# Roots of the key head norms, spread over the partitions by DMAs through a DRAM scratch in place of 16 selector products

## The reference, cut to what matters

```
def macaron_half(x, g, w_in, w_out):
    a, b = jnp.split(rms_norm(x, g) @ w_in, 2, axis=-1)
    return x + 0.5 * ((jax.nn.silu(a) * b) @ w_out)

def memory_kv(mem, g_mem, w_mkv, g_km):
    km, vm = jnp.split(rms_norm(mem, g_mem) @ w_mkv, 2, axis=-1)
    km = rms_norm(km.reshape(B, M, H_MEM, HEAD_DIM), g_km)
...
    k = rms_norm(k.reshape(B, S, H_A, 2, HEAD_DIM), p['g_k'])      # layer 0 keys, 12 heads of 64
...
    kb = rms_norm(kb.reshape(B, S, H_B, HEAD_DIM), g_kb)           # shared keys of layer 1, 12 heads of 64
```

## Time and profile before

| what | value |
|---|---|
| median of 3 runs | 1270.58 us (1270.34 to 1271.26) |
| span of the profiled execution, first to last instruction | 1269.0 us |
| PE busy | 1259.1 us, 99% |
| DVE busy | 753.9 us, 59% |
| ACT busy | 561.3 us, 44% |
| POOL busy | 187.3 us, 15% |
| DMA, mean rate over the span | 148 GB/s |

### The profile page before, as it was taken

How to read it: one execution, slowest core, us unless ns; L and a number is a source line. 1 busy time by engine, 2 the same in 40 slices (tenths; PEclk the granted TensorE clock), 3 DMA queues, 4 the chain that set the end, 5 groups by cost and what they waited for, 6 DMA issues and landing times.

```text
span 1269.0 us, 22398 instructions
## 1 busy us (share of the span) xinstructions
PE 1259.1 (99%) x8772; PEld 1241.4 (98%) x8772; DVE 753.9 (59%) x1135; ACT 561.3 (44%) x829; POOL 187.3 (15%) x206
## 2 busy tenths in 40 slices
PE   9999999999999999999999999999999999999999
PEld 8999999999998999999999999999997899999999
DVE  7766575555677656564555775554456765656433
ACT  6543453344276543433353443333355754343322
POOL 0120021146143000000122000001134420000000
PEclk9999999999999999999999999999999999999999
DMA  8364445643204443454443534354440134443343
GB/s 307 135 180 137 166 145 169 212 173 133 100 35 147 148 166 132 165 171 142 146 170 119 198 133 158 140 166 161 157 167 34 68 133 166 136 162 138 131 141 128
DMA packets 38829, 187.64 MB, mean 148 GB/s; under 512 B 4432, under 2 KB 13008, under 8 KB 23664
## 3 DMA queue, kind: packets, MB, share of 16 engines
q1 hardware_dynamic: 37296, 183.43, 41.7%
q0 software_dynamic: 1184, 3.13, 1.2%
q10 hardware_dynamic: 288, 0.24, 0.1%
HBM read 179.89 MB, written 6.90 MB: 147 GB/s over the span
## 4 chain that ended last, share of the span: by engine, by line
PE 97%; ACT 1%; DVE 1%; DMA 0%; issue 0%; SPq 0%; DVEq 0%; ACTq 0%
PE bank L504 30%; PE bank L506 30%; PE bank L505 30%; PE bank L918 1%; PE bank L780 1%; PE bank L741 1%; PE bank L783 1%; PE bank L750 1%; DMA raw<-in_w_ffn_in 0%; PE outs L530 0%; ACT ew L1321 0%; PE outs L532 0%; PE bank L552 0%; PE outs L817 0%; PE bank L545 0%
## 5 line engine op out<-in xcount | busy, mean ns | idle before, releaser
L504 PE MATMUL bank<-xhi,whi 128*128 128x320 f32 (+1 forms) x1760 | 545.8, 310 | 1.2 <-DVE wlo L1949 1.2
L506 PE MATMUL bank<-xhi,wlo 128*128 128x320 f32 (+1 forms) x1760 | 543.0, 309 | 0.0
L505 PE MATMUL bank<-xlo,whi 128*128 128x320 f32 (+1 forms) x1760 | 543.0, 309 | 0.0
L1562 DVE TENSOR_TENSOR wlo<-raw,whi 128x2048 fp32r<-128x2048 f32 (+1 forms) x176 | 361.5, 2054 | 235.7 <-ACT whi L1155 235.6
L1155 ACT ACTIVATE whi<-raw 128x2048 fp32r<-128x2048 f32 (+1 forms) x177 | 304.4, 1720 | 330.7 <-PE bank L506 325.0
L504 PEld LDWEIGHTS bank<-xhi,whi 128*128 128x128 f32 x1760 | 330.6, 188 | 3.7 <-issue 1.8
L505 PEld LDWEIGHTS bank<-xlo,whi 128*128 128x128 f32 x1760 | 330.7, 188 | 0.5
L506 PEld LDWEIGHTS bank<-xhi,wlo 128*128 128x128 f32 x1760 | 330.6, 188 | 0.0
L504 PE MATMUL bank<-hhi,whi 128*128 128x320 f32 x704 | 217.8, 309 | 0.0
L506 PE MATMUL bank<-hhi,wlo 128*128 128x320 f32 x704 | 217.5, 309 | 0.0
L505 PE MATMUL bank<-hlo,whi 128*128 128x320 f32 x704 | 217.5, 309 | 0.0
(11 more groups left out here) (236 smaller groups left out, 1051.7 us busy)
## 6 DMA issues: line engine op xcount, KB each, us to landing
raw<-in_w_ffn_in SPq DMA_DIRECT2D x85, 1024.0 KB, 4.8
raw<-in_w_ffn_out SPq DMA_DIRECT2D x64, 704.0 KB, 4.1
raw<-in_w_in_a SPq DMA_DIRECT2D x10, 1024.0 KB, 4.7
raw<-in_w_out SPq DMA_DIRECT2D x8, 1024.0 KB, 4.8
raw<-in_w_kv SPq DMA_DIRECT2D x6, 1024.0 KB, 4.7
raw<-in_w_mkv SPq DMA_DIRECT2D x4, 1024.0 KB, 4.8
raw<-in_w_in_b SPq DMA_DIRECT2D x4, 1024.0 KB, 4.8
raw<-in_w_ffn_in SPq DMA_DIRECT2D x6, 256.0 KB, 6.5
```

The lines of the kernel that those rows point to most:

```text
L504: mm(acc, wh, mhi(ks[q]), start=start and q == 0, stop=False)
L505: mm(acc, wh, mlo(ks[q]), start=False, stop=False)
L506: last = mm(acc, wl, mhi(ks[q]), start=False, stop=stop and q == nk - 1)
L1562: tt(wlo[slot][:, 0:size], raw[slot][:, 0:size], f32(whi[slot][:, 0:size]), ALU.subtract).then_inc(lo_ready[slot], 1)
```

## The change

The roots of the four sets of keys (`ROWS`: mkv0, mkv1, pa_k, kv) no longer pass through `rs` and PE. DVE writes them in full to `rt0`. ACT then issues one DMA that stores them in a DRAM scratch (`rows_to_memory`) and, after that has landed, two DMAs that read each row back onto 64 partitions (`rows_from_memory`). `head_scale` multiplies with that SBUF tile. `early_rows` lies in the buffer of `pt`, `late_rows` in the region of `qz`. A new semaphore `k_scaled` counts scaled key tiles. The stores of the memory keys and values wait for it and move in SP's order, and the scaling of the memory keys moves from d = 1 and 3 to d = 3 and 7 of `out0`.

```diff
+ROWS = {"mkv0": (0, 2, N_MEM), "mkv1": (1, 2, N_MEM), "pa_k": (2, 6, R), "kv": (3, 6, R)}
+SCALED = {"mkv0": 0, "mkv1": 2, "pa_k": 4, "kv": 10}
...
 (SP)
-            load_stage("out0", 0, 4)
-            for layer in range(2):
+            load_stage("out0", 0, 5)
+            def store_memory(layer):
                 st = f"mkv{layer}"
-                sp.wait_ge(aux_free, AUX0[st] + 4)
+                sp.wait_ge(k_scaled, SCALED[st] + 2)
+                sp.wait_ge(aux_free, AUX0[st] + 2)
                 store(a["o_mkT"][layer].rearrange("(k p) r -> p k r", p=P), kmT[:, layer])
                 store(a["o_mv"][layer].rearrange("(k p) r -> p k r", p=P), vm[:, layer])
-                if layer == 0:
-                    load_stage("out0", 4, 6)
+            store_memory(0)
+            load_stage("out0", 5, 6)
             sp.dma_start(ckT[:], a["cakT"]...)
             sp.dma_start(cv[:], a["cav"])...
             load_stage("out0", 6, 7)
...
             load_stage("out0", 7)
-            load_stage("pa")
+            load_stage("pa", 0, 1)
+            store_memory(1)
+            load_stage("pa", 1)
...
-            sp.wait_ge(aux_free, AUX0["dec"])
+            sp.wait_ge(k_scaled, SCALED["kv"] + 6)
             store(a["o_bkT"].rearrange("(k p) r -> p k r", p=P), kbT[:])
 (PE)
-                else:
-                    head_broadcast(st, AUX0[st] + 2, N_MEM)
...
-                if 11 <= j < 14:
-                    head_broadcast("pa_k", AUX0["pa_k"] + 2 * j - 22, R, [2 * j - 22, 2 * j - 21])
...
-                if i == 2 and j < 3:
-                    head_broadcast("kv", f + 7 + 2 * j, R, [2 * j, 2 * j + 1])
 (ACT)
+            def rows_to_memory(hn):
+                n, tiles, w = ROWS[hn]
+                act.wait_ge(hr_ready, HNORM[hn][0] + 1)
+                act.dma_start(rows_out[n, 0:2 * tiles, 0:w], rt0[0:2 * tiles, 0:w]).then_inc(d_rows_out, 16)
+
+            def rows_from_memory(hn):
+                n, tiles, w = ROWS[hn]
+                act.wait_ge(d_rows_out, 16 * (n + 1))
+                for e in range(2):
+                    src = bass.AP(rows_out.tensor, (12 * n + e) * R, [[0, HD], [2 * R, tiles], [1, w]])
+                    dst = rows_of(hn)[HD * e:HD * e + HD, :]
+                    act.dma_start(dst.rearrange("p (t r) -> p t r", t=tiles), src).then_inc(d_rows, 16)
...
+                       after=lambda j: rows_to_memory("mkv0") if j == 3 else None)
+            def memory_rows(d):
+                if d == 1:
+                    rows_from_memory("mkv0")
+                    head_root("mkv1", N_MEM)
+                if d == 3:
+                    rows_to_memory("mkv1")
+                if d == 5:
+                    rows_from_memory("mkv1")
...
+            def key_rows(hn):
+                def after(j):
+                    if j == 9:
+                        rows_to_memory(hn)
+                    if j == 10:
+                        rows_from_memory(hn)
+                return after
 (DVE)
                 val = tmp[0]
+                if hn in ROWS:
+                    stt(out=val[0:64, 0:w], in0=v, scalar=-3.0, in1=half, ...).then_inc(hr_ready, 1)
+                    return
...
+            def head_scale(hn, dst, g, tiles):
+                dve.wait_ge(d_rows, 32 * (ROWS[hn][0] + 1))
+                for j in tiles:
+                    stt(out=dst(j), in0=dst(j), scalar=g(j), in1=row_tile(hn, j), ...).then_inc(k_scaled, 1)
...
             def left_mkv(d):
+                if d in (3, 7):
+                    layer = d // 4
+                    head_scale(f"mkv{layer}", lambda j: kmT[:, layer, j, :], ..., range(2))
...
-                if 11 <= j < 14:
-                    head_scale("pa_k", ..., [2 * j - 22, 2 * j - 21])
+                if 13 <= j < 16:
+                    head_scale("pa_k", ..., [2 * j - 26, 2 * j - 25])
```

More of the change, by code:

```diff
@@ L82 @@
 AUX0 = {"mkv0": 0}
-AUX0["mkv1"] = AUX0["mkv0"] + 2 + 2
-AUX0["pa_k"] = AUX0["mkv1"] + 2 + 2
-AUX0["pa_q"] = AUX0["pa_k"] + 6
+AUX0["mkv1"] = AUX0["mkv0"] + 2
+AUX0["pa_q"] = AUX0["mkv1"] + 2
 AUX0["pa_v"] = AUX0["pa_q"] + 4
@@ L89 @@
 AUX0["kv"] = AUX0["pa_m"] + 2
-AUX0["dec"] = AUX0["kv"] + 1 + 6 + 1 + 6
+AUX0["dec"] = AUX0["kv"] + 1 + 6 + 1
+ROWS = {"mkv0": (0, 2, N_MEM), "mkv1": (1, 2, N_MEM), "pa_k": (2, 6, R), "kv": (3, 6, R)}
+SCALED = {"mkv0": 0, "mkv1": 2, "pa_k": 4, "kv": 10}
 AUX0["pb_m"] = AUX0["dec"] + 2
@@ L196, in encoder_kernel @@
         with ExitStack() as region:
+            sb("lower", [P, 8 * R], F32, region)
+            late_rows = sb("late_rows", [P, 6 * R], F32, region)
+        with ExitStack() as region:
             sb("under", [P, 4 * 640], F32, region)
@@ L215, in encoder_kernel @@
         idd = sb("idd", [P, HD])
+        early_rows = pt[:].rearrange("p a b -> p (a b)")
         hsq = sb("hsq", [P, R])
@@ L262, in encoder_kernel @@
         zT = qk[0:H_B, 13, :]
+        rows_out = nc.dram_tensor("rows_out", [4, 12, R], F32, kind="Internal").ap()
         scratch = nc.dram_tensor("bias_scratch", [64, H_A, NREL + 1], F32, kind="Internal").ap()
@@ L289, in tile_b, with row_tile, rows_of @@
             return qk[:, 6 + j, :] if j < 2 else qk[:, j - 2, :]
+        def row_tile(hn, j):
+            n, tiles, w = ROWS[hn]
+            return rows_of(hn)[:, j * w:(j + 1) * w]
+        def rows_of(hn):
+            n, tiles, w = ROWS[hn]
+            if hn == "kv":
+                return late_rows[:]
+            return early_rows[:, 512 * n:512 * n + tiles * w] if n < 2 else early_rows[:, 0:tiles * w]
         def pair_of(column):
@@ L377, in encoder_kernel @@
         d_out = sem("d_out")
+        d_rows_out = sem("d_rows_out")
+        d_rows = sem("d_rows")
+        k_scaled = sem("k_scaled")
         const_loads = [(select, a["select"]), (late, a["late"]), (hot, a["hot"]), (table, a["table"]),
@@ L1482, in _ @@
             nc.scalar.activation(lam[:, 2:4], lam[:, 0:2], ACT.Exp).then_inc(lam_exp, 1)
-            projection("mkv1", N_MEM, [("mkv1", 0)], 4, lambda j: kmT[:, 1, j, :], {1: "mkv0"})
-            ffn_out("out0", "attn_0", "pa", lambda d: head_root("mkv1", N_MEM) if d == 1 else None)
+            projection("mkv1", N_MEM, [("mkv1", 0)], 4, lambda j: kmT[:, 1, j, :], {1: "mkv0"},
+                       after=lambda j: rows_to_memory("mkv0") if j == 3 else None)
[7 more added lines that the diff above has]
+                    rows_from_memory("mkv1")
+            ffn_out("out0", "attn_0", "pa", memory_rows)
             exps_a, attention_a = attention(0)
             exps_b, attention_b = attention(1)
+            def key_rows(hn):
[5 more added lines that the diff above has]
+                return after
             def before_last(j):
@@ L1497, in _ @@
             projection("pa", R, [("pa_k", 0), ("pa_q", 6), ("pa_m", 18)], 20, tile_a, {7: "pa_k", 13: "pa_q"}, True,
-                       before=before_last)
+                       before=before_last, after=key_rows("pa_k"))
             attention_a()
@@ L1506, in _ @@
             nc.scalar.activation(wfs[:], wf[:], ACT.Copy).then_inc(wf_hi_ready, 1)
-            projection("kv", R, [("kv", 0)], 12, lambda j: kbT[:, j, :], {7: "kv"})
+            projection("kv", R, [("kv", 0)], 12, lambda j: kbT[:, j, :], {7: "kv"}, after=key_rows("kv"))
             act.wait_ge(kv_half, 1)
@@ L1596, in head_root @@
                 val = tmp[0]
+                if hn in ROWS:
+                    stt(out=val[0:64, 0:w], in0=v, scalar=-3.0, in1=half, op0=ALU.add, op1=ALU.mult).then_inc(hr_ready, 1)
+                    return
                 stt(out=val[0:64, 0:w], in0=v, scalar=-3.0, in1=half, op0=ALU.add, op1=ALU.mult)
@@ L1599, in head_root @@
                 tt(rs[32:64, 0:w], val[32:64, 0:w], f32(rs[32:64, 0:w]), ALU.subtract).then_inc(hr_ready, 1)
[L1601 to L1605, removed]
+            def head_scale(hn, dst, g, tiles):
+                dve.wait_ge(d_rows, 32 * (ROWS[hn][0] + 1))
+                for j in tiles:
+                    stt(out=dst(j), in0=dst(j), scalar=g(j), in1=row_tile(hn, j), op0=ALU.mult, op1=ALU.mult
+                        ).then_inc(k_scaled, 1)
             def query_blocks(src, t, g, scale, used=aux_free):
@@ L1991, in left_mkv @@
             def left_mkv(d):
+                if d in (3, 7):
+                    layer = d // 4
+                    head_scale(f"mkv{layer}", lambda j: kmT[:, layer, j, :], lambda j: hgain(f"km{layer}"), range(2))
                 if d > 3:
@@ L1999, in left_mkv @@
                     take_values(AUX0[st], 2, [(0, P), (P, P)], lambda c: vm[:, layer, c, :])
-                else:
-                    head_scale(st, AUX0[st] + 2, lambda j: kmT[:, layer, j, :], lambda j: hgain(f"km{layer}"), N_MEM)
                 if d == 1:
@@ L2024, in after_pa @@
             def after_pa(j):
-                if 11 <= j < 14:
-                    head_scale("pa_k", AUX0["pa_k"] + 2 * j - 22, lambda k: qk[:, 6 + k, :], lambda k: hgain("ka"), R,
```

(5 more changed lines are left out.)

## The result

The changed kernel takes 1280.02 us (median of 5 runs, 1279.09 to 1280.27) against 1270.58 us (1270.06 to 1271.26) before: 9.4 us slower, ratio 1.0071 with a 95% interval of 1.0060 to 1.0082. The forecast of 1275.6 us had the sign and the places right and was 4.4 us too low, and the time lies outside its range (1273.2 to 1278.4).

The account below looks back on a forecast made before the run. The prediction took PE, busy 99% of the span, as the bound. Its terms, -2.2 for products, +4.8 and +2.4 for two stalls, gave +5.0 us: span 1274.0, time 1275.6 us, range 1273.2 to 1278.4.

Parts of the forecast that it names:

- The gain of the products: PE: four 256-column and twelve 320-column products removed, giving back 2.2 us, 0.17% of the kernel.
- nothing under 0.2% can be: Whole kernel: below 0.2% no measurement can tell a change from none.
- DVE's and ACT's shares: DVE's dropped root operations put at nothing; ACT's 12 DMA issues hidden behind its waits for PE.
- row stores and row reads: pa and kv: ACT's wait for the store counted as nothing, the two 480 KB reads taken as in time.
- the two rows weighed: Landing of the row reads: 384 KB from DRAM scratch in 7.8 us, 1 MB of weights in 4.7 us.
- The rival of late reads: pa, tile 13: reads one after the other hold DVE some 5 us, 3 us more, 1278.6; chance 0.06.
- The first place: out0, d = 5: SP's store wait delays pair 5's load; PE stalls 4.8 us, between 3.7 and 5.5.
- The second place: pa, tile 4: pair 1's load goes out behind the second store; PE stalls 2.4 us, between 1.3 and 3.5.
- The clock: Rival: PE's clock falls once in the 4.8 us stall, 2.2 us more, 1277.8 us; chance 0.20.
- The sum: Whole kernel: -2.2 + 4.8 + 2.4 = +5.0 us, time 1275.6 us.
- The argument against it: Against a fall of the clock in the stall: nothing in this trace ever fell.
- the price of 2.2 us: Kernel start: 15 matmuls of 320 columns take 4.37 us, against 0.147 us each later: 2.2 us more.

Follow-up runs that it names:

- order_both: Changed kernel with the memory stores moved behind pair 5 of out0 and behind pair 1 of pa: 1268.26 us, ratio to before 0.9982.
- products_x3: Kernel before with each of the 16 products done three times into the same bank: 1275.27 us.
- order_out0: Changed kernel with only the first memory store moved, behind pair 5 of out0: 1272.70 us, ratio to before 1.0017.
- scale_early: Changed kernel, same SP order, with DVE scaling the memory keys at the end of d = 2 and 6 instead of 3 and 7: 1267.98 us.
- before_late_load: Kernel before with the store of layer 1's memory keys ahead of pair 5 of out0 instead of pair 6: 1277.23 us, ratio 1.0049.
- square_first: Changed kernel with ACT's square of tile 1 of pa ahead of its rounding of pair 1: 1278.86 us, ratio to before 1.0063.
- keep_warm: Changed kernel with 28 filler products ahead of d = 5 in out0 and 20 behind tile 3 of pa: 1276.63 us.

## Why the prediction was wrong, point by point

**The gain of the products** was right: 2.2 us forecast, 2.2 (order_both) and 2.3 (half of products_x3) measured.

**The gain could be told**, though the prediction held that nothing under 0.2% can be: 11 executions against 28 gave 0.9973 to 0.9991 for order_both.

**DVE's and ACT's shares, row stores and row reads** were right in costing nothing. The reads of 480 KB landed 7.0 and 8.5 us after their issue, the slow end of the two rows weighed. They overlapped, as was assumed, so that the second landed 1.8 us before DVE began to use them at 330.93. The rival of late reads did not occur, but the margin was thin: ACT issued the first read 10.9 us ahead of that use (forecast 10.6), and 9.1 of them passed until the second had landed.

**The first place** was right in mechanism and size: 4.8 us forecast, 4.5 in the profile. order_both, order_out0 and scale_early show that it is the wait, and before_late_load that the order of SP suffices for it.

**The second place** was right about the late load and wrong about who keeps PE waiting. The prediction looked at ACT's square of tile 2, which delays slot 1, and rightly found that in time. In ACT's stream the rounding also stands ahead of the square of tile 1, and PE needs the remainder of that one earlier, at the end of tile 3. POOL then took 2.52 us for it beside DVE's conversion, where 0.88 would have been in time. Forecast 2.4 us, measured 3.3. square_first took away that detour.

**The clock** is the step that failed. The sum stood at full clock, and the fall was a rival with a chance of 0.20, counted once with 2.2 us. It fell in both places, behind each of the two stalls in every profile in which one was left open, and cost 2.2 + 1.2 = 3.4 us. keep_warm gave back 3.4 us. With it the forecast would have been 1275.6 + 3.4 = 1279.0, and with the second stall 0.9 us longer and the first 0.3 shorter 1279.6, against 1280.02 measured. The argument against it, that nothing in the trace ever fell, was empty: that trace has no wait of PE over 1.3 us, so nothing in it could have shown a fall. The matmuls at half pace at the start show how slow PE can be, and not what makes it so: the 1.26 us of idle time ahead of them are no longer than a wait of 1.27 us at 386.93 that left the pace alone, and what lies ahead of the span is not in the trace. The granted clock doesn't show this stretch at all (kernel before, columns as above):

```profile
0.00:5.00 5.00, 3.74 (x14) 3.74 (x15) 1.58 (x6) 2.43 (x4) 0.19 (x4) 1.00 0.62 178
```

So "full from end to end" was read from a column that misses the start, and the price of 2.2 us matches the first stall's by luck: it was taken from a duration (4.37 us), where the starts of the 15 matmuls and the next one, at 5.48, are 4.22 us apart and give 2.0. The Trainium skill ("TensorE: Matmul & The Clock Gate", section "Part 1: The HAM clock gate") says that the array falls back to half rate after an idle stretch, and by that rule a fall was to be expected. The traces agree, with 0.50 and 0.52 granted in the stretches behind the stalls of 4.5 and 3.3 us.

## What to carry to other kernels

A store in a hand-ordered DMA stream holds up every load behind it until its wait is met. When a step that such a store waits for is moved later, look up when each load behind it could have gone, and move the store behind those or the step ahead. If PE is the bound, price each new stall of PE at its own length plus the half clock behind it, once for each stall: in the profiles here 1.2 to 2.7 us behind stalls of 2.5 to 4.5 us, and none behind waits of 1.3 us. And follow every engine that holds the late block in its stream: the work queued behind it may reach PE before the block itself does.

## What was not expected of the hardware

The clock also fell behind a wait of 2.4 us, and after PE was back at work. In square_first PE was idle for 2.4 us, began tile 4 at full rate, and fell to half rate some 0.7 us later:

```profile
291.35 0.30 PE L531 MATMUL bank<-xlo,whi 128*128 128x320 f32 x1
291.50 0.31 PE L532 MATMUL bank<-xhi,wlo 128*128 128x320 f32 x1
...
292.26 0.47 PE L530 MATMUL bank<-xhi,whi 128*128 128x320 f32 x1
292.53 0.47 PE L531 MATMUL bank<-xlo,whi 128*128 128x320 f32 x1
```

The time at half clock differs between profiles at the same place: after the stall at d = 5 it ended at 246.2 in the changed kernel (4.7 us after PE began again), at 246.6 in before_late_load (3.0 us), and at 247.3 in square_first (5.8 us), whose program is that of the changed kernel up to there. The loss was 2.2, 1.4 and 2.7 us, a spread of over 1 us in the cost of one stall. And in two of the eleven executions of order_out0 the mean clock stayed at 1.000.
